# The shared keys and values of the second block: norm sums ahead of the bias products, the products inside the projection, the seventh layer's norm spread out, and the key spreading between value tiles

## The reference, cut to what matters

```python
...
        x = x + 0.5 * swiglu_ffn(x, ffn_post_norm[layer], ffn_post_w_in[layer], ffn_post_w_out[layer])
        if layer == N_A_LAYERS - 1:
            k_blocks, v_blocks = shared_kv_blocks(x, kv_norm, kv_w, kv_k_norm)
```

## Time and profile before

| | |
|---|---|
| median of three runs | 2795.89 us (2795.7 to 2798.36) |
| the profiled execution's own time | 2800.63 us |
| its span, first to last instruction | 2798.8 us |
| TensorE busy | 2712.5 us, 97% of the span |
| VectorE, ScalarE, GpSimd busy | 2045.9, 1011.9, 145.8 us |
| mean granted TensorE clock | 0.984 |

### The profile page before, as it was taken

The page is one execution under the profiler, slowest core; times in us unless marked ns, Lnnn a source line. Parts: engine busy times, 40 slices in busy tenths (PEclk is TensorE's granted clock), DMA queues, the critical chain, the costliest instruction groups (busy, mean ns, idle before and its releaser), DMA issues.

```text
span 2798.8 us, 48948 instructions
## 1 busy us (share of the span) xinstructions
PE 2712.5 (97%) x19262; PEld 2415.7 (86%) x19262; DVE 2045.9 (73%) x3070; ACT 1011.9 (36%) x1169; POOL 145.8 (5%) x206
## 2 busy tenths in 40 slices
PE   6999999999999999999999999998999999999999
PEld 4888878888888888888799999977799989996999
DVE  5988887777787766776667776766777776675677
ACT  4222234222242222343443544452144443443443
POOL 1000011000010000100010000000000000000000
PEclk9999999999999999999999999999999999997999
DMA  9455532444434444232254445421045555543354
GB/s 359 163 190 180 181 136 94 161 150 150 159 120 148 160 150 149 97 106 91 72 195 180 164 178 190 179 76 47 3 174 193 194 129 183 192 165 68 123 193 180
DMA packets 68706, 421.44 MB, mean 151 GB/s; under 512 B 7672, under 2 KB 8824, under 8 KB 26592
## 3 DMA queue, kind: packets, MB, share of 16 engines
q1 hardware_dynamic: 48176, 343.36, 33.4%
q0 software_dynamic: 20432, 76.69, 8.7%
HBM read 418.95 MB, written 1.07 MB: 150 GB/s over the span
## 4 chain that ended last, share of the span: by engine, by line
PE 88%; DVE 8%; ACT 2%; issue 1%; DMA 1%; SPq 0%; ACTq 0%; DVEq 0%
PE ps_o L2309 11%; PE ps_o L2310 11%; PE ps_o L2311 10%; PE ps_g L2309 8%; PE ps_u L2309 8%; PE ps_u L2310 8%; PE ps_u L2311 8%; PE ps_g L2310 8%; PE ps_g L2311 8%; DVE wlo L1319 2%; PE ps_o L2553 1%; DMA scr<-in_AW 1%; PE ps_o L2539 1%; DVE tsq L1372 1%; PE ps_u L2530 1%
## 5 line engine op out<-in xcount | busy, mean ns | idle before, releaser
L787 ACT ACTIVATE whi<-wraw 128x2048 fp32r<-128x2048 f32 x314 | 598.9, 1911 | 773.5 <-PE ps_u L2311 343.8
L1319 DVE TENSOR_TENSOR wlo<-wraw,whi 128x2048 fp32r<-128x2048 f32 x314 | 711.6, 2287 | 120.6 <-ACT whi L787 120.4
L2309 PE MATMUL ps_g<-hh,wlo 128*128 128x256 f32 (+1 forms) x1464 | 464.0, 317 | 4.0 <-DVE hl L1385 3.4
L2310 PE MATMUL ps_u<-hl,whi 128*128 128x256 f32 (+1 forms) x1464 | 463.0, 316 | 0.0
L2309 PE MATMUL ps_u<-hh,wlo 128*128 128x256 f32 (+1 forms) x1464 | 462.9, 316 | 0.0
L2310 PE MATMUL ps_g<-hl,whi 128*128 128x256 f32 (+1 forms) x1464 | 462.8, 316 | 0.0
L2311 PE MATMUL ps_u<-hh,whi 128*128 128x256 f32 (+1 forms) x1464 | 462.1, 316 | 0.0
L2311 PE MATMUL ps_g<-hh,whi 128*128 128x256 f32 (+1 forms) x1464 | 462.0, 316 | 0.0
L2309 PE MATMUL ps_o<-ah,wlo 128*128 128x256 f32 (+1 forms) x1360 | 434.9, 320 | 5.7 <-DVE x L1425 5.7
L2310 PE MATMUL ps_o<-al,whi 128*128 128x256 f32 (+1 forms) x1360 | 433.8, 319 | 0.0
L2311 PE MATMUL ps_o<-ah,whi 128*128 128x256 f32 (+1 forms) x1360 | 432.9, 318 | 0.0
(11 more groups left out here) (494 smaller groups left out, 3757.5 us busy)
## 6 DMA issues: line engine op xcount, KB each, us to landing
wraw<-in_W SPq DMA_DIRECT2D x315, 1024.0 KB, 4.9
scr<-in_ADA POOLq DMA_DIRECT2D x126, 512.0 KB, 4.1
scr<-in_AW SPq DMA_DIRECT2D x5, 1024.0 KB, 26.5
big<-in_AW SPq DMA_DIRECT2D x4, 1024.0 KB, 15.6
scr<-bias_rows POOLq DMA_DIRECT2D x8, 384.0 KB, 8.2
x<-in_XT SPq DMA_DIRECT2D x1, 2048.0 KB, 10.5
x<-in_MEMT POOLq DMA_DIRECT2D x2, 1024.0 KB, 7.4
cst<-in_CST POOLq DMA_DIRECT2D x1, 1511.5 KB, 7.5
```

The costliest lines, as they stand in the source:

```text
L787: nc.scalar.activation(whi[:, n % SLOTS, :], wraw[:, n % SLOTS, :], ACT.Copy).then_inc(w_hi, 1)
L1319: tt_(wlo[:, n % SLOTS, :], wraw[:, n % SLOTS, :], whi[:, n % SLOTS, :].bitcast(f32), sub).then_inc(w_lo, 1)
L2309: mm(out, a[1], b[0], start=first, stop=False)
L2310: mm(out, a[0], b[1], start=False, stop=False)
```

## The change

Five edits, all in the kv stage. (1) TensorE sums the squares first; the bias products move into `project_first`, behind the products of the sixth of eight rows, and use banks 0, 1 and 3. (2) DVE adds the bias behind its norm, into `hid` instead of `scr`; the wait for the stored rows (`bi_dram`) moves from the head of the stage to the key squares, which write `hid`. (3) Of the seventh FFN's norm, rows 0 to 3 stay behind kv+0, rows 4 and 5 behind kv+1, rows 6 and 7 go behind kv+4. (4) The six spreading products become three pairs, ahead of kv+5's first tile, ahead of its second, and in the middle of the second. (5) The keys are scaled pair by pair, the last two pairs between kv+5's copies.

The hunks below are, in this order, the buffers, ScalarE's list, DVE's and TensorE's; the three short ones ahead of the last are the new hooks in `project_first`, `project_tokens` and `head_spread`.

```diff
-        rowb = scr[0:4, 3072:4608]
+        rowb = hid[0:4, 0:1536]
...
+        AGAIN_ROWS = {0: range(4), 1: range(4, 6), 4: range(6, KT)}
+        BIAS_BANKS = BANK[0], BANK[1], BANK[3]
...
                 split_hi(n + c + SLOTS)
-                if c in (0, 1):
-                    norm(lambda d: x[:, d, :], NX, None, "split", None, FIRST["kv", 0], again=True, o=NX, rows=range(4 * c, 4 * c + 4))
                 if c == 3:
                     head_norm()
+                if c in AGAIN_ROWS:
+                    norm(lambda d: x[:, d, :], NX, None, "split", None, FIRST["kv", 0], again=True, o=NX, rows=AGAIN_ROWS[c])
...
+            norm(xs_, NX, gain("kv_norm_2"), None, "split")
             dve.wait_ge(bi_row, 1)
             for g in range(3):
-                tt_(rowb[:, 512 * g:512 * (g + 1)], BANK[1 + g][0:4, :], bt[0:4, 1536 + 512 * g:2048 + 512 * g], add).then_inc(bi_sb, 1)
-            norm(xs_, NX, gain("kv_norm_2"), None, "split")
+                tt_(rowb[:, 512 * g:512 * (g + 1)], BIAS_BANKS[g][0:4, :], bt[0:4, 1536 + 512 * g:2048 + 512 * g], add).then_inc(bi_sb, 1)
...
                 if q == 1:
-                    if c in (0, 1):
-                        norm(xs_, NX, gain("ffn_pre_norm_2", 1), None, "split", again=True, o=NX, rows=range(4 * c, 4 * c + 4))
                     if c == 2:
+                        dve.wait_ge(bi_dram, 16)
                         head_squares((k_g, V("kv_k_norm_2")))
                     elif c == 3:
                         head_factors()
-                    elif c == 4:
-                        head_scale((k_g, V("kv_k_norm_2")))
-
-            dve.wait_ge(bi_dram, 16)
+                    if c in AGAIN_ROWS:
+                        norm(xs_, NX, gain("ffn_pre_norm_2", 1), None, "split", again=True, o=NX, rows=AGAIN_ROWS[c])
+                    if c == 4:
+                        scale_keys(range(1))
+                if c == 5 and q == 0:
+                    scale_keys(range(1, 3))
+
+            def scale_keys(pairs):
+                for j in pairs:
+                    st["back"] += 1
+                    dve.wait_ge(hn_back, st["back"])
+                    keys = k_g[:, 2 * j:2 * j + 2, :]
+                    ins = stt(keys, keys, V("kv_k_norm_2"), BANK[j].rearrange("p (k n) -> p k n", n=NX), mult, mult)
+                if pairs[-1] == 2:
+                    ins.then_inc(hn_done, 1)
...
+                    if then is not None and k == KT - 3:
+                        then()
...
+                        if between is not None:
+                            between(q, k)
...
-                for i in range(nt):
+                for i in range(nt) if only is None else (only, only + 1):
...
-            pe.wait_ge(bias_in, 32)
-            for g in range(3):
-                ins = mm(BANK[1 + g][0:4, :], rel[:, 4 * g:4 * g + 4], bt[:, 512 * g:512 * (g + 1)], start=True, stop=True)
-            ins.then_inc(bi_row, 1)
-            pe.wait_ge(bi_sb, 3)
+            def bias_rows_():
+                pe.wait_ge(bias_in, 32)
+                for g in range(3):
+                    ins = mm(BIAS_BANKS[g][0:4, :], rel[:, 4 * g:4 * g + 4], bt[:, 512 * g:512 * (g + 1)], start=True, stop=True)
+                ins.then_inc(bi_row, 1)
+
+            def spread_pair(q, k):
+                if (q, k) in ((0, 0), (1, 0), (1, 4)):
+                    head_spread(6, only=2 * (q + k // 4))
+
             norm(NX, idle=0)
             memory_sums(1)
-            project_first(FIRST["kv", 0], NX)
+            project_first(FIRST["kv", 0], NX, then=bias_rows_)
             project(FIRST["kv", 0] + 2, NX)
             project_tokens(FIRST["kv", 0] + 3, NX)
             head_sums(6, idle=0)
             project_tokens(FIRST["kv", 0] + 4, NX)
-            head_spread(6)
-            project_tokens(FIRST["kv", 0] + 5, NX)
+            project_tokens(FIRST["kv", 0] + 5, NX, between=spread_pair)
             pe.wait_ge(hn_done, st["hn"])
```

More of the change, by code:

```diff
@@ L2397, in project, with project_first @@
                         then(j)
-            def project_first(n, N, of=None, count=2):
+            def project_first(n, N, of=None, count=2, then=None):
                 ready = split_input(of or N)
@@ L2411, in project_first, with project_tokens @@
                                 ins.then_inc(mm_done, 1)
-            def project_tokens(n, ntok, t0=0):
+                    if then is not None and k == KT - 3:
+                        then()
+            def project_tokens(n, ntok, t0=0, between=None):
                 w = weights(chunk(n), 256)
@@ L2504, in head_sums, with head_spread @@
                 ins.then_inc(hn_sum, 1)
-            def head_spread(nt, banks=BANK):
+            def head_spread(nt, banks=BANK, only=None):
                 pe.wait_ge(hn_inv, st["hn"])
-                for i in range(nt):
+                for i in range(nt) if only is None else (only, only + 1):
                     ins = mm(third(banks, i), C("spread", 1024)[0:16, 128 * i:128 * (i + 1)], head_rows, start=True, stop=True)
```

## The result

The changed kernel is slower: 2809.74 us (median of five runs, 2804.15 to 2813.14) against 2798.36 for the kernel before, run beside it (five runs, 2795.7 to 2800.78). The ratio is 1.0042, with a 95% interval of 1.0031 to 1.0052. The prediction (2793.3, range 2790.3 to 2798.0) was wrong, sign and range. It had started from 2795.89, the median of three runs of before; from 2798.36 its -2.6 us would give 2795.8, and that misses as clearly.

A forecast was written before the change was run, and what follows sets the result against it. TensorE, busy 97% of the span, was taken as the bound, with some 10 us of losses in the stage. Terms -2.45 + 2.75 - 1.67 - 1.2 = -2.6 us took 2795.89 to 2793.3 us, range 2790.3 to 2798.

The forecast's parts named there:

- The transfers: Bias loads issued about 19 us later meet kv+6's and kv+7's weight loads: cost taken as 0, bound 5.7 us.
- the bias loads hold up the weights: Rival: late kv+6 and kv+7 weights make TensorE wait at `hn_done`; 2796.6 or 2799.0 us; chance 0.2.
- The start of the projection: Start of the kv stage: sums no longer wait for DVE's additions; gain 2.45 us, bounds -0.15 and 3.85.
- The bias products inside the projection: Same six passes, now with nothing to hide in: cost 2.75 us, up to 1.5 more if the clock falls.
- Two norm rows fewer behind kv+1: Key squares end earlier, so TensorE's 2.41 us stop for them shrinks to 0.75: gain 1.67 us.
- The spreading in pairs: Late kv stage: no long thin stretch, so no half clock behind it; gain 1.2 us, bounds -0.3 and 1.2.
- The end of the stage: Wait for `hn_done` ahead of `ffn(6)`: cost 0, with 0.5 us at most to spare.
- The sum: All terms together: -2.6 us; from the end of `ffn(5)` to `ffn(6)`'s first product 54.9 us instead of 57.5.

The follow-up runs named there:

- experiment 1: Changed kernel with the four bias loads issued one by one in the seventh layer instead of inside the kv stage: 2796.93 us, 1.0006 of before.
- experiment 2: Kernel before with the four bias loads held until the products of kv+1 are done: 2807.51 us, 1.0034 of before.
- experiment 6: Changed kernel with only the third and fourth bias load put off into the seventh layer: 2798.97 us, 1.0005 of before.
- experiment 7: Changed kernel with each bias load issued only when the one before it has landed: 2797.25 us, 1.0001 of before.
- Experiment 5: Changed kernel with the root of the head norm ahead of kv+6's split on ScalarE instead of behind it: 2804.4 us, 1.0023 of before.
- Experiment 9: Changed kernel with the four bias loads issued by ScalarE, behind its part of kv+1's norm rows, instead of by GpSimd: 2801.98 us, 1.0008 of before.
- Experiment 4: Kernel before with only parts (3) to (5) of the change, the start of the stage as before: 2797.53 us, 0.9995 of before.
- experiment 11: The changed kernel itself, measured once more on another occasion against the kernel before: 2811.27 us, 1.0047 of before.
- experiment 3: Changed kernel with bias products back ahead of the norm sums, in banks those don't use, additions and bias loads as before: 2794.88 us, 0.9988 of before.
- experiment 8: Kernel before with only parts (1) and (2) of the change, norm rows and six spreads as before: 2807.2 us, 1.0033 of before.

## Why the prediction was wrong, by its own steps

**The transfers** is the step that failed: taken as 0, bounded at 5.7. It took the one weight load of before that met the bias loads, 11.0 us, as what a load that meets them costs. That load had been issued at 2255.9, some 9.5 us behind the last of the four bias loads (2243.35 + 3.05 = 2246.4); it had met the end of them. kv+6's was issued at 2268.0, 2.6 us behind the last of them (2262.37 + 3.06), met almost all, and took 16.8. TensorE would have stood a landing up to about 2279.4 (2284.8 less the wait of 5.37). Experiments 1, 2, 6 and 7 show the cause by taking the loads away, adding them, halving them and spacing them. The prediction also put the place wrong: it looked for the wait at `hn_done`, by way of kv+7. The root queued behind kv+6's split brought it to the first pair already. Experiment 5 shows that without that order most of it comes at `hn_done` after all.

The trace of before held the number that was needed. The 12.1 us of the earlier trace rows is the median of four loads that landed one after the other; the last, issued at 2245.6, has this row:

```profile
scr<-bias_rows POOLq DMA_DIRECT2D x1, 384.0 KB, 18.8
```

So the four together were done at 2264.5, 21.1 us behind the issue of the first, and the weight load behind them landed 2.5 us later (2255.9 + 11.0 = 2266.9). Carried over to a first issue at 2262.37, that is an end of the bias loads at 2283.5 (measured 2283.1) and kv+6's weights at about 2286 (measured 2284.8). The prediction's own path needed them by 2277.3 (the first pair at 2281.5 less 1.91 + 0.5 + 1.74).

**The rival "the bias loads hold up the weights"** (chance 0.2, 2796.6 or 2799.0) had the mechanism and the sign, and was too small. Its smaller price, weights getting every other turn, was the Trainium skill's rule ("DMA: Bandwidth & Descriptors", section "Queues, rings and completion order"). The trace doesn't agree here: 206 packets of the bias queue and none of the weights in 6 us. Nor did the load of 11.0 us, which the prediction took as agreeing, take turns in its first 3 us (before, 2255.8 to 2259):

```profile
q0 software_dynamic: 60, 0.20, 78.0%
q1 hardware_dynamic: 3, 0.02, 12.7%
```

Its landing agreed in size only. Experiment 9 is in between: nothing at first, then both queues at once.

**The start of the projection**: gain 2.45 forecast, bounds -0.15 and 3.85. The projection began 10.39 us behind `ffn(5)` in place of 11.99, a gain of 1.60, with 6.8 us at half clock. In experiments 1, 5 and 9, whose TensorE list is the same up to there, it was 9.7 us with 3.4 at half; in 6 and 7 it was 8.3 us with none. The gain thus reads as 1.6 to 3.7, but the 11.99 of before has a clock of its own: 6.8 us at half. Experiment 4, with the same start as before, took 12.14 with 6.8 at half, and experiment 2 took 10.98 with 3.4. With as much half clock on both sides the gain is 1.3 to 1.9 (10.98 less the 9.68 of experiment 1, and less the 9.07 of experiment 11). Whether the new start also gets a better clock is not shown: its eight profiles have 0 to 6.8 us at half, the three of the old start 3.4 to 6.8.

**The bias products inside the projection**: 2.75 forecast. From the projection's begin to the stop ahead of kv+3's first tile it took 18.45 us before (2266.10 - 2247.65), 21.10 in experiments 1, 5, 6, 7 and 9 (+2.65). In the changed kernel it was 22.43, with 3.4 us of half clock right behind the products: the "up to 1.5 more", here 1.33. Why the clock falls behind these products in some executions (both profiles of the changed kernel, and experiment 8) and not in the five others with the same products in the same place, stays open.

**Two norm rows fewer behind kv+1**: forecast 1.67. From that stop to the head sums it took 8.32 us before (2274.42 - 2266.10) and 6.68 after (2275.04 - 2268.36): 1.64. Right.

**The spreading in pairs**: forecast 1.2. Without the collision the end of the stage is 9.36 us instead of 10.10: 0.74. The half clock is gone as foreseen, the pairs themselves cost some 0.5 more than the 0.3 I gave them.

**The end of the stage**: no wait for `hn_done` in the changed kernel or in experiments 1, 3, 4, 6 and 7. Right, as long as kv+6 is in time.

**The sum** without the transfers was -2.6 and a stage of 54.9 us. Experiments 1, 6 and 7 have 55.4, 54.5 and 54.0. So in the stage the other terms came out near their sum, with less from the start and the pairs than forecast and the rest from the clock. In whole-run time these three kernels are level with before (1.0006, 1.0005, 1.0001) rather than 0.1% under it, and the forecast's gain is not shown. What lies outside the stage varies by more than that from one execution to the next (from the first product of `ffn(6)` to the end of the span 502.7 us in experiment 1, 505.7 before, 507.6 in experiment 6). But the lean is one way: in eleven of the twelve comparisons the ratio amounts to 1 to 6 us more than the stage's difference from 57.4. The 57.4 is one profile with 10.2 us of half clock, and may be longer than the stage of before usually is; whether it is that, or something outside the stage gives time back, stays open.

**Where the 8.4 us went** in the changed kernel's profile: start -1.60, bias products +2.65 and half clock behind them +1.33, norm rows -1.64, the wait at the pair +5.44, the end +2.19 (12.29 us from the first spread to `ffn(6)` in place of 10.10, with 6.8 us of half clock behind the wait). Together +8.37; the stage's difference is 65.80 - 57.42 = 8.38.

## What to carry to other kernels

When an edit moves a producer, follow its transfers to the moment when they will now be issued, and ask which load will be issued just behind them and who stands in line behind that load's consumer: here the root of another computation stood behind a weight split on the same engine. A landing time read from a trace holds for that load's distance from the transfers it met, not for any load that meets them; and a median over a burst hides when the burst ends, which is what the load behind it waits for. Where a burst of loads isn't urgent, issuing one when the last has landed keeps the line short, and cost nothing that could be measured here (1.0001); and work that fills a wait that is there anyhow, like the bias products before, is free until it is moved.

## What was not expected of the hardware

Behind loads on GpSimd's queue the weights, on another queue, had to wait for what was issued ahead of them: weights issued 2.6 us behind four bias loads moved nothing for 6 us (changed kernel), and one load at a time took the engines in turn with the weights, each after the other (experiment 7). Weights issued 1.3 us ahead of four such loads on ScalarE's queue landed in 5.0 us as if alone (experiment 9). Behind those loads the weights moved nothing for 8 us and then went along with them, and landed 5.5 us ahead of the last. So the order of issue decided who came first with both queues, but only behind GpSimd's loads was it kept to the end.

The same instruction list on TensorE was granted full clock or half clock at the start of the stage from one kernel to the next (0, 3.4 or 6.8 us at half), worth 2.1 us of the stage (10.39 against 8.27 to the projection's begin), with a stop of 2.7 us ahead of it in every one.
